# First projection on unnormed X, its scale applied on leaving PSUM, and the relative bias made at the start

## The reference

```python
def rmsnorm(x, g):
    x32 = x.astype(jnp.float32)
    y = x32 * lax.rsqrt(jnp.mean(x32 * x32, axis=-1, keepdims=True) + EPS)
    return (y * g.astype(jnp.float32)).astype(x.dtype)

def conformer_conv(h, w_pw1, b_pw1, w_dw, b_dw, ln_g, ln_b, w_pw2, b_pw2):
    u = h @ w_pw1 + b_pw1
    a, gate = jnp.split(u, 2, axis=-1)
    u = a * jax.nn.sigmoid(gate)
    u = lax.conv_general_dilated(...) + b_dw      # causal, depthwise, 31 taps
    u = jax.nn.silu(layernorm(u, ln_g, ln_b))
    return u @ w_pw2 + b_pw2
```

## Time and profile before

| | us |
|---|---|
| median of 3 runs | 1744.09 (1743.7 to 1745.18) |
| the profiled execution | 1744.05 |
| its span, first to last instruction | 1742.2 |

### The profile page before, as it was taken

The page is one execution under the profiler, slowest core; times in us unless marked ns, Lnnn a source line. Parts: engine busy times, 40 slices in busy tenths (PEclk is TensorE's granted clock), DMA queues, the critical chain, the costliest instruction groups (busy, mean ns, idle before and its releaser), DMA issues.

```text
span 1742.2 us, 24232 instructions
## 1 busy us (share of the span) xinstructions
PE 1713.0 (98%) x9506; PEld 1430.2 (82%) x9506; DVE 1205.4 (69%) x1652; ACT 833.2 (48%) x1380; POOL 273.4 (16%) x207
## 2 busy tenths in 40 slices
PE   9999999999999999999999999999999999999998
PEld 6885889889988787799889988766678778888887
DVE  6998789549955555889459956569636676536753
ACT  6876555325633443556226534555654444214432
POOL 2994200000001000200000013672201200000002
PEclk9999999999999999999999999999999999999998
DMA  4210422312231311222412332422112123222321
GB/s 182 95 55 25 127 93 102 137 59 108 98 136 70 129 67 37 93 95 98 157 49 98 118 131 90 146 89 87 61 50 92 68 82 115 91 73 96 107 98 49
DMA packets 28948, 163.45 MB, mean 94 GB/s; under 512 B 4607, under 2 KB 7947, under 8 KB 12460
## 3 DMA queue, kind: packets, MB, share of 16 engines
q1 hardware_dynamic: 25664, 156.28, 25.3%
q10 hardware_dynamic: 3180, 5.74, 1.1%
HBM read 154.65 MB, written 4.47 MB: 91 GB/s over the span
## 4 chain that ended last, share of the span: by engine, by line
PE 84%; DVE 7%; POOL 6%; ACT 2%; issue 1%; DMA 0%; POOLq 0%; ACTq 0%; DVEq 0%
PE PSUM L738 19%; PE PSUM L740 18%; PE PSUM L739 18%; PE PSUM L1007 7%; PE PSUM L1008 7%; PE PSUM L1009 7%; POOL CV L2200 4%; DVE W_lo L2339 1%; POOL ISC L2264 1%; DVE WK L2930 1%; PE PSUM L1243 1%; PE PSUM L1264 1%; PE PSUM L1255 1%; PE PSUM L1094 0%; DVE H_lo L2312 0%
## 5 line engine op out<-in xcount | busy, mean ns | idle before, releaser
L738 PE MATMUL PSUM<-H_hi,W_hi 128*128 128x512 f32 x1056 | 426.0, 403 | 7.7 <-DVE W_lo L2339 2.9
L740 PE MATMUL PSUM<-H_hi,W_lo 128*128 128x512 f32 x1056 | 411.9, 390 | 0.0
L739 PE MATMUL PSUM<-H_lo,W_hi 128*128 128x512 f32 x1056 | 411.9, 390 | 0.0
L1449 ACT ACTIVATE W_hi<-W_raw 128x2048 fp32r<-128x2048 f32 (+1 forms) x96 | 181.9, 1895 | 318.9 <-PE PSUM L740 318.9
L2339 DVE TENSOR_TENSOR W_lo<-W_raw,W_hi 128x2048 fp32r<-128x2048 f32 (+1 forms) x96 | 237.3, 2472 | 71.8 <-ACT W_hi L1449 42.3
L2152 POOL TENSOR_TENSOR SSUM<-SSUM,SQ 128x512 f32<-128x512 f32 x43 | 62.5, 1454 | 1303.6 <-ACT SQ L1516 1301.8
L738 PEld LDWEIGHTS PSUM<-H_hi,W_hi 128*128 128x128 f32 x1056 | 198.3, 188 | 69.3 <-issue 21.2
L740 PEld LDWEIGHTS PSUM<-H_hi,W_lo 128*128 128x128 f32 x1056 | 198.2, 188 | 42.5
L739 PEld LDWEIGHTS PSUM<-H_lo,W_hi 128*128 128x128 f32 x1056 | 198.5, 188 | 37.2 <-issue 1.0
L738 PE MATMUL PSUM<-HID_hi,W_hi 128*128 128x512 f32 x480 | 187.3, 390 | 1.5 <-DVE HID_lo L2504 1.4
L739 PE MATMUL PSUM<-HID_lo,W_hi 128*128 128x512 f32 x480 | 186.8, 389 | 0.0
(11 more groups left out here) (412 smaller groups left out, 3475.5 us busy)
## 6 DMA issues: line engine op xcount, KB each, us to landing
W_raw<-in_inp SPq DMA_DIRECT2D x13, 1024.0 KB, 4.8
W_raw<-in_pw SPq DMA_DIRECT2D x11, 1024.0 KB, 4.8
W_raw<-in_gu0a SPq DMA_DIRECT2D x11, 1024.0 KB, 4.8
W_raw<-in_gu0b SPq DMA_DIRECT2D x11, 1024.0 KB, 4.8
W_raw<-in_gu1a SPq DMA_DIRECT2D x11, 1024.0 KB, 4.8
W_raw<-in_gu1b SPq DMA_DIRECT2D x11, 1024.0 KB, 4.8
W_raw<-in_gu2a SPq DMA_DIRECT2D x11, 1024.0 KB, 4.8
W_raw<-in_gu2b SPq DMA_DIRECT2D x11, 1024.0 KB, 4.8
```

The lines of the kernel that those rows point to most:

```text
L738: nc.tensor.matmul(dst[:], wh, x_hi[:, k, :], start=(k == first), stop=False)
L739: nc.tensor.matmul(dst[:], wh, x_lo[:, k, :], start=False, stop=False)
L740: return nc.tensor.matmul(dst[:], wl, x_hi[:, k, :], start=False, stop=(k == last))
L1449: i = nc.scalar.activation(W_hi[b][:, 0:n], W_raw[b][:, 0:n], ACT.Copy)
```

## The change

Five things, all ahead of the layer norm:

- X is multiplied as it is. ACT makes `H_hi` from X and the gain as each pair of tiles lands, DVE `H_lo`; `normed` goes. The sum of squares and its spread are made beside unit 0 and unit 1, and DVE copies the spread from PSUM into `R`.
- Per unit DVE multiplies value and gate by `R` out of PSUM, the value into `U`, the gate into `GATE`. The sigmoid then reads and writes `GATE`, and the last step multiplies `U` by it in place. Two taps of the convolution stand between.
- The loads are all on SP's queue, X and weights in turn. The weights of units 0 and 1 are split in halves. For units 1 to 6 ACT splits the weights of the unit after next ahead of the sigmoid, not behind it.
- The table of the relative bias is loaded and multiplied at the start.
- PE takes 7 taps of tile 6 from DVE: 59 taps against 119. DVE does 0, 6, 6, 7, 6, 7, 6 taps behind units 0 to 6, and 2 ahead of the last step of units 1 to 7, where that tile is there.

```diff
-PE_TILES = [(4, 0), (6, 10)]
+PE_TILES = [(4, 0), (6, 3)]
...
-DVE_TILES = [(0, 8, CONV_WIDTH), (2, 0, CONV_WIDTH), (3, 0, CONV_WIDTH), (6, 0, 10), (7, 0, CONV_WIDTH)]
-DVE_TAPS = [12] * 7
+DVE_TILES = [(0, 8, CONV_WIDTH), (2, 0, CONV_WIDTH), (3, 0, CONV_WIDTH), (6, 0, 3), (7, 0, CONV_WIDTH)]
+DVE_TAPS = [0, 6, 6, 7, 6, 7, 6]
...
+TAPS_BESIDE_GATE = 2
...
         @block.sync
...
+            first_tiles(0)
             sp.dma_start(W_raw[0][:, 0:FIRST_COLS], a["pw1"][0][:, 0:FIRST_COLS]).then_inc(first_in, 16)
+            first_tiles(1)
             sp.dma_start(W_raw[0][:, FIRST_COLS:2 * FIRST_COLS], a["pw1"][0][:, FIRST_COLS:2 * FIRST_COLS]).then_inc(raw_in[0], 16)
+            first_tiles(2)
+            first_tiles(3)
             load(order[0], a["pw1"], At(1))
...
         @block.tensor
...
-            zero_products(4)
-            pe.wait_ge(const_in, 16)
-            first_sum()
+            zero_products(3)
+            bias_products()
             zero_products(1)
-            pe.wait_ge(r_made, MIX0 + 1)
-            token_spread(AUX[1], r_ps)
-            zero_products(3)
             for k in range(L.kt):
...
+                if k == 5:
+                    pe.wait_ge(const_in, 16)
+                    first_sum(0)
+            first_sum(1)
             for j in range(1, L.n):
...
+                        if (j, half, k) == (1, 0, 1):
+                            pe.wait_ge(r_made, MIX0 + 1)
+                            pe.wait_ge(fvec_made, 3)
+                            token_spread(AUX[1], r_ps)
             for n in range(len(PE_TAPS)):
                 conv_tap(n)
-                if n == PE_ENDS[0] + 5:
-                    bias_products()
...
         @block.scalar
...
+            act.dma_start(onehot[:], a["onehot"]).then_inc(tab_in, 16)
+            act.dma_start(table[0:BUCKETS, :], a["rel_bias"]).then_inc(tab_in, 16)
             warm_table(ACT.Sqrt)
...
+            act.wait_ge(x_in[0], 16)
+            first_hi(0)
+            first_hi(1)
+            act.wait_ge(first_in, 16)
+            first_weights(0, 0, w_half)
+            first_square(0)
+            first_square(1)
...
+            first_weights(1, 1, w_hi)
+            for g in range(3):
+                take_bias(g)
             token_std(MIX0)
...
+            split_hi(act, layers["pw1"], At(0))
...
             def glu_gate(j):
 
-                act.wait_ge(acc_ready, 2 * j + 2)
-                if j >= 2:
-                    act.wait_ge(glu_made, j - 1)
-                nc.scalar.activation(GATE[j % 2][:], PS[2 * (j % 2) + 1][:], ACT.Sigmoid, bias=vec("b_pw1", At(DT + j))).then_inc(gate_act, 1)
+                act.wait_ge(glu_in, j + 1)
+                nc.scalar.activation(GATE[j % 2][:], GATE[j % 2][:], ACT.Sigmoid, bias=vec("b_pw1", At(DT + j))).then_inc(gate_act, 1)
...
             for j in range(L.n):
+                if 0 < j < L.n - 1:
+                    split_hi(act, L, At(j))
                 glu_gate(j)
                 if j < L.n - 1:
-                    split_hi(act, L, At(j))
...
         @block.vector
...
+            def first_h_lo(m):
 
                 dve.wait_ge(h_hi_made, m + 1)
-                nc.vector.scalar_tensor_tensor(out=H_lo[:, m, :], in0=CV[:, m, :], scalar=vec("norm_mix0", m),
+                nc.vector.scalar_tensor_tensor(out=H_lo[:, m, :], in0=X[:, m, :], scalar=vec("norm_mix0", m),
...
+            nc.vector.tensor_copy(R[:], AUX[1][:]).then_inc(r_copied, 1)
...
             for j in range(L.n):
+                value = U[:, j, HALO:HALO + SEQ]
+                dve.wait_ge(acc_ready, 2 * (L.base + j) + 1)
+                nc.vector.tensor_tensor(value, PS[2 * (j % 2)][:], R[:], ALU.mult).then_inc(glu_value, 1)
                 dve.wait_ge(acc_ready, 2 * (L.base + j) + 2)
+                nc.vector.tensor_tensor(GATE[j % 2][:], PS[2 * (j % 2) + 1][:], R[:], ALU.mult).then_inc(glu_in, 1)
+                conv(TAPS_BESIDE_GATE, j)
                 dve.wait_ge(gate_act, j + 1)
-                nc.vector.scalar_tensor_tensor(out=U[:, j, HALO:HALO + SEQ], in0=PS[2 * (j % 2)][:], scalar=vec("b_pw1", j),
+                dve.wait_ge(glu_value, VALUE0 + j + 1)
+                nc.vector.scalar_tensor_tensor(out=value, in0=value, scalar=vec("b_pw1", j),
                                                in1=GATE[j % 2][:], op0=ALU.add, op1=ALU.mult).then_inc(glu_made, 1)
                 if j < L.n - 1:
                     split_lo(L, At(j))
```

More of the change, by code:

```diff
@@ L796, in zero_products, with first_sum @@
                     nc.tensor.matmul(PS[2][:], ZERO[:, 0:P], ZERO[:], start=True, stop=True)
[L798 to L804, removed]
-                    if k < DT // 2 - 1:
-                        zero_products(1)
-                last.then_inc(stat_ready, 1)
+            def first_sum(part):
+                pe.wait_ge(ss_made, (3, 6)[part])
+                for b in range(4):
+                    last = nc.tensor.matmul(AUX[0][:, b:b + 1], tokens(FIRST_SQ[(0, 4)[part]], b), ones[:, 0:1],
+                                            start=(part == 0 and b == 0), stop=(part == 1 and b == 3))
+                if part:
+                    last.then_inc(stat_ready, 1)
             def idle_products(bank, n):
@@ new lines, in _ @@
+            first_weights(0, 1, w_hi)
+            first_square(2)
+            first_square(3)
+            act.wait_ge(x_in[2], 16)
+            first_hi(4)
+            first_hi(5)
+            first_square(4)
+            act.wait_ge(x_in[3], 16)
+            first_hi(6)
+            first_hi(7)
+            act.wait_ge(raw_in[1], 16)
+            first_weights(1, 0, w_half)
+            first_square(5)
+            first_square(6)
+            first_square(7)
+            first_weights(1, 1, w_hi)
@@ L1645, in _ @@
             split_hi(act, L, At(L.n - 1))
-            for g in range(3):
-                take_bias(g)
-            act.wait_ge(fvec_made, 3)
-            act.dma_start(bias_rows.rearrange("(g h) d -> h g d", h=GROUP_HEADS), fvec[:]).then_inc(rows_out, 16)
             warm_table(ACT.Sqrt)
@@ L2398, in normed_lo, with first_w_lo, first_pair @@
                                                in1=H_hi[:, m, :].bitcast(F32), op0=ALU.mult, op1=ALU.subtract).then_inc(h_lo_made, 1)
-            for k in range(DT // 2):
+            def first_w_lo(u, half, made):
+                cols = slice(half * FIRST_COLS, half * FIRST_COLS + FIRST_COLS)
+                nc.vector.tensor_tensor(W_lo[u][:, cols], W_raw[u][:, cols], W_hi[u][:, cols].bitcast(F32),
+                                        ALU.subtract).then_inc(made, 1)
+            def first_pair(k):
@@ new lines, in _ @@
+            first_pair(0)
+            first_h_lo(2)
+            first_h_lo(3)
+            dve.wait_ge(w_hi, 1)
+            first_w_lo(0, 1, w_lo)
+            first_pair(1)
+            first_h_lo(4)
+            first_h_lo(5)
+            two_pairs(0, 2)
+            first_h_lo(6)
+            first_h_lo(7)
+            dve.wait_ge(w_half, 2)
+            first_w_lo(1, 0, first_lo)
+            first_pair(2)
+            first_pair(3)
+            two_pairs(2, 5)
+            dve.wait_ge(w_hi, 2)
@@ L2403, in _ @@
+            first_w_lo(1, 1, w_lo)
             dve.wait_ge(std_made, MIX0 + 1)
             nc.vector.reciprocal(R4[:], STD4[:]).then_inc(r_made, 1)
[L2405 to L2411 removed]
```

116 lines of the change are left out of this document (47 added, 69 removed).

## The result

| | us |
|---|---|
| before, median | 1744.15 |
| after, median of 4 runs | 1760.66 (1760.35 to 1762.16) |
| ratio | 1.0096, 95% interval 1.0078 to 1.0113 |
| the profiled execution, and its span | 1760.87, 1759.1 |

What follows compares the result with a forecast made beforehand. Three nearly equal lists on PE, DVE and POOL were taken as the bound, POOL ending last by a little. Waits for tile 2 move the sums' end from 151.19 to 158.9: 1744.05 + 7.7 = 1751.8 us, range 1746.5 to 1755.5.

Steps and rivals of the forecast that it cites:

- the bias at nothing: PE's bias products, 2.1 us, were counted at nothing at start and end, since PE is waiting at the start anyway.
- the slip: If the bias table landed late, PE's start at 9.1 us would slip by as much.
- the start: PE starts at 9.1, 10.3 us earlier; unit 0's last step on DVE ends at 28.6, 4.3 us earlier.
- The collisions: DVE's splits and last steps collide with POOL ahead of tile 2's end: 6.3 us taken, between 2.7 and 10.
- The prediction's 111: DVE's tile 2 would end at 111 if every unit's last step paid up to 0.57 us for excluding POOL.
- Who waits for tile 2: POOL waits about 9 us for DVE's tile 2; PE some 11 before its first tap, 2 to 3 before tile 6.
- Rival (d): PE's clock slows after its long wait, in the taps of tile 4; at 8 us loss 1.3, 1753.1; chance 0.07.
- (b): Faster, 1739.8, if only the start mattered; the change gains if DVE's tile 2 ends below 99.8; chance 0.08.
- the whole 4.3 us: POOL's list begins 4.3 us earlier, at unit 0's last step; the gain is kept only if tile 2 ends at 95.5.

Runs made afterwards that it cites:

- the bias late: Changed kernel with the bias's loads and products back behind the eight units, between PE's tiles 4 and 6, and six zero products at the start: 1755.45 us.
- Eight taps a unit: Changed kernel with DVE doing 8 taps behind each of the first seven units instead of 0, 6, 6, 7, 6, 7, 6: 1754.54 us.
- the sigmoid first: Changed kernel with ACT's split of weights back behind the sigmoid in units 1 to 6: 1759.06 us.
- 1747.24: Changed kernel with the bias in unit 0, the value scaled in PSUM and 8 DVE taps behind each of the first seven units: 1747.24 us.
- 1743.07: Kernel with bias in unit 0, value in PSUM and 8 DVE taps, POOL's second low part moved from tap 18 to tap 10 of tile 5: 1743.07 us.
- three edits together: Changed kernel with the bias in unit 0, POOL adding tile 2 later and making PE's first low part earlier, and the value scaled in PSUM: 1749.81 us.

## Why the prediction was wrong

The forecast against the trace of the changed kernel, each row from the rows above:

| | forecast | measured | gap |
|---|---|---|---|
| first real product | 9.1 | 13.86 | 4.8 |
| last step of unit 0 ends | 28.6 | 34.81 | 6.2 |
| unit 1 ends on DVE | 40.3 | 46.83 | 6.5 |
| tile 2 ends | 107.5 | 115.89 | 8.4 |
| PE's first tap | 110.2 | 118.77 | 8.6 |
| PE's tile 6 begins | 134.7 | 143.67 | 9.0 |
| the sums end | 158.9 | 167.87 | 9.0 |

**The step that failed** is the one that counted the bias at nothing "at either end (at the start PE is waiting anyway; if the table landed late, PE's start at 9.1 would slip by as much)". It was 6.2 of the 9.0 us. The table is 1.5 KB, issued on ACT's queue at 2.34 and landed at 9.48: I had no row for such a load beside the full queues and took it for done. It did not stand there alone. Ahead of it on the same queue are a constant, and the matrix of zeros and ones that the bias needs, too (issues of the first 12 us, by size):

```profile
onehot<-in_onehot ACTq DMA_DIRECT2D x1, 148.5 KB
cmat<-in_cmat ACTq DMA_DIRECT2D x1, 128.0 KB, 6.3
table<-in_rel_bias ACTq DMA_DIRECT2D x1, 1.5 KB
```

By their sizes, the packets of the constant run to 6.55 us in the trace, those of the matrix to 8.12 and those of the table to 8.75. So what had to be reckoned with was a load of some 280 KB beside X and the weights, not one of 1.5. The price that I named, the slip, was itself too small: 0.4 us of slip (9.48 against 9.1), 3.3 for the bias (9.48 to 12.77), 1.1 for the product of zeros behind it (to 13.86), and 1.9 for the first six real products, which took 3.26 us (to 17.12) and not 6 x 0.23. That is 6.7; the rest of unit 0 took 0.5 less than forecast. The kernel with the bias late shows the step apart from the rest: its unit 0 ends at 28.14, 6.7 earlier, and its time is 5.2 lower.

**Of the start, the rest held**: from the first product to the end of unit 0's last step that kernel took 19.3 us (8.88 to 28.14), and 19.5 were forecast (9.1 to 28.6).

**The sigmoid of unit 6** cost 1.7 us that I did not have. ACT makes that unit's sigmoid behind twelve diagonals, four scaled copies and the split of weights, much as in unit 1, which I did work out (2.7 and 3.8; measured 2.79 and 2.81); I stopped at unit 1. Eight taps a unit hide it, and with the sigmoid first it is gone.

**The collisions were sized rightly**: from the end of unit 1 to that of tile 2 the trace has 115.89 - 46.83 - 1.70 = 67.4, the forecast 60.9 + 6.3 = 67.2. The six splits took 18.1 (20.4 less the first, 2.29) against 13.2 alone. Of the six last steps the longest took 1.74, more than the 1.32 of the earlier trace rows (as did the 1.61 of unit 1), and three the 0.74 of an undisturbed one. That the sum comes out within 0.2 is in part luck: 6.3 was a middle taken between 2.7 and 10, for a collision at every unit, where four splits of six took the full 1.1 more. (The prediction's 111 for 0.57 at every last step doesn't follow from its own terms: 101.2 + 2.4 + 6 x 0.57 is 107.) By the Trainium skill ("SBUF — State Buffer", the list under the ports' diagram) a DVE instruction with two SBUF inputs and a POOL instruction that reads SBUF shut each other out; the runs agree in that the last steps are undisturbed when one operand is in PSUM (0.749 each). The splits, which have two inputs in SBUF whatever the last step has, come down from 2.91 to 2.71 in the mean with it, not to the 2.28 of one alone.

**Who waits for tile 2** held step by step: POOL 12.12 us (9 forecast; tile 2 itself was later), PE 11.5 (11) and 1.17 (2 to 3), and PE the last to finish. (In the kernel before it was PE, too: its sums wait for nothing in the earlier trace rows, and it needs POOL's tile 5, done at 149.52, only for the last of them, from about 150.2. POOL's own end is the latest there, as the prediction says, but nothing waited for it.) Rival (d) came true in this place and cost nothing: the clock was at its lower level from PE's wait of 11.5 us until 122 to 123, and 31 taps took 23.7 us where 21.8 were forecast, inside PE's wait ahead of tile 6. The same mechanism at the start, behind 2.6 us, was not covered by anything, and there I had not looked for it.

**The rival on the other side** (b) named the end of tile 2 as the point from which it decides, below 99.8. The eight taps bring it to 100.5 and the time stays 10 us above the kernel before, as three lists must be served. With the bias in unit 0 and the value in PSUM as well it ended at 94.4, below the 95.5 at which the whole 4.3 us were to be kept, and the time was still 3.0 above: the end of tile 2 does not decide alone. Where tile 2 ended at 92.5, with the bias out of the start, the value in PSUM, eight taps a unit and POOL's second low part early, the kernel was 3 us faster than before; so the earlier start can be kept in part, and what was kept of it is 3 us, not 10.

What stays open: how much of the 4.2 us between 1747.24 and 1743.07 is PE's clock, beyond the estimate above; how early the table would land ahead of the 280 KB on its queue, which no run tried; and how much of the 3 us could be had with X normed first, as no run balanced the lists of the kernel before anew.

## What to carry to other kernels

Work that is put into an engine's wait must have its own inputs by then: ask when its load lands beside all others and behind what its own queue carries, and keep the filler ahead of it and not behind, so that the engine is never idle when the real work is about to come. When several engines' hand-ordered lists end within a few microseconds of each other, removing the one wait that the profile shows moves the end to the next list (12 us of it here for nothing), and an edit that looks worthless alone can pay beside others. Look at the clock before calling it worthless: here a new wait at the join had brought the lower level, which took 2.25 us of what the edit gave. Before a result is scaled in place in SBUF, see whether it can stay in PSUM: the instruction that reads it next may collide with another engine's.

## What the runs showed of the hardware

- A load of 1.5 KB, behind some 280 KB on its own queue and among the loads of the first 12 us, 3.5 MB in all, landed 7.1 us after its issue (2.34 to 9.48), and differently from run to run: the bias began at 9.48, 9.20, 8.82, 9.15 and 10.11 in five kernels with the same start.
- The granted clock can fall after the engine has taken up work again: after a wait of 2.61 us it was 1.00 for another 0.7 us, and then 0.50 for 6.8 us; after one of 3.70 us it was 0.99 in the second window and 0.50 in the next three. It can also fall within the wait: in the run of three edits together, where PE waited 3.66 us, it was 0.77 in the window ahead of the one in which PE took up work. After 0.22, 1.17 and 1.47 us it stayed at 1.00.
- An operand's place can decide an instruction's time: a last step of 0.75 us took up to 1.74 with both operands in SBUF beside POOL, and 0.749 in the mean with one of them in PSUM. A split of 2.28 us, both of its inputs in SBUF, took up to 3.38 beside POOL.
